# Products of the first token half placed between the two halves of a norm, at five seams of a two-block transformer

## What is computed

```
h = rms_norm(x, g_pre) * (1 + scale) + shift        # modulate
y = sublayer(h)                                      # products with large weights
x = x + res_w * (1 + gate) * rms_norm(y, g_post)     # residual_add
```

## Time and profile before

| | us |
|---|---|
| median of 3 runs (1696.91 to 1699.64) | 1698.38 |
| the profiled execution | 1699.22 |
| its span, first to last instruction | 1697.4 |

### The profile page before, as it was taken

One profiled execution on the slowest core, in us unless ns is written; L12 is line 12 of the kernel. 1 busy time (PEld: TensorE's weight loads), 2 busy tenths in 40 slices (PEclk: granted clock), 3 DMA queues, 4 the chain that ended last, 5 costly groups with the idle time before them and its releaser, 6 DMA issues.

```text
span 1697.4 us, 29607 instructions
## 1 busy us (share of the span) xinstructions
PE 1659.9 (98%) x12344; PEld 1550.8 (91%) x12344; DVE 1266.7 (75%) x1852; ACT 873.8 (51%) x1215; POOL 21.7 (1%) x39
## 2 busy tenths in 40 slices
PE   3999999999999999999999999999999999999998
PEld 3999899988999899989999988999899989989997
DVE  7777889987878677676877765887677686778553
ACT  4555466654544365666464334534355676473432
POOL 0000000000000000000000000000000000000000
PEclk9999999999999999999999999999999999999999
DMA  9878756786777745755558786777945846547542
GB/s 377 319 256 253 268 198 218 208 329 244 295 285 277 294 154 195 223 182 207 208 199 286 284 223 237 246 279 288 287 154 199 221 177 224 212 176 259 198 162 100
DMA packets 71079, 398.80 MB, mean 235 GB/s; under 512 B 8225, under 2 KB 8737, under 8 KB 36385
## 3 DMA queue, kind: packets, MB, share of 16 engines
q1 hardware_dynamic: 67968, 387.43, 65.1%
q0 software_dynamic: 2976, 9.47, 1.6%
HBM read 395.79 MB, written 1.08 MB: 234 GB/s over the span
## 4 chain that ended last, share of the span: by engine, by line
PE 83%; DVE 6%; ACT 5%; DVEq 2%; DMA 1%; issue 1%; SPq 1%; ACTq 0%
PE att L695 19%; PE lin L518 18%; PE lin L519 18%; PE lin L520 18%; DVE lo L1312 3%; ACT hi L922 2%; PE att L802 2%; PE lin L558 1%; PE lin L560 1%; PE lin L568 1%; DVEq L1678 1%; PE att L852 1%; DMA ada_s<-in_ada 1%; ACT work L942 1%; PE pt L829 1%
## 5 line engine op out<-in xcount | busy, mean ns | idle before, releaser
L1312 DVE TENSOR_TENSOR lo<-raw,hi 128x2048 fp32r<-128x2048 f32 x269 | 615.5, 2291 | 254.1 <-ACT hi L922 253.4
L518 PE MATMUL lin<-h_hi,hi 128*128 128x256 f32 x2448 | 688.3, 281 | 1.4 <-DVE work L1673 1.0
L520 PE MATMUL lin<-h_hi,lo 128*128 128x256 f32 x2448 | 683.3, 279 | 0.0
L519 PE MATMUL lin<-h_lo,hi 128*128 128x256 f32 x2448 | 683.3, 279 | 0.0
L922 ACT ACTIVATE hi<-raw 128x2048 fp32r<-128x2048 f32 x269 | 513.3, 1912 | 191.4 <-PE att L695 99.6
L518 PEld LDWEIGHTS lin<-h_hi,hi 128*128 128x128 f32 x2448 | 460.1, 188 | 4.1 <-issue 3.9
L519 PEld LDWEIGHTS lin<-h_lo,hi 128*128 128x128 f32 x2448 | 460.3, 188 | 0.1
L520 PEld LDWEIGHTS lin<-h_hi,lo 128*128 128x128 f32 x2448 | 460.1, 188 | 0.0
L1325 DVE CUSTOM_DVE_ANT_0 ada_w<-ada_w,cs 128x1024 f32<-128x1024 f32 x179 | 217.8, 1219 | 11.9 <-DMA ada_w<-in_ada 11.7
L1162 ACT ACTIVATE work<-lin 128x256 f32<-128x256 f32 x88 | 33.8, 384 | 269.2 <-PE lin L520 268.2
L695 PE MATMUL att<-hi,act_lo 128*128 128x512 f32 x440 | 138.8, 389 | 0.0
(11 more groups left out here) (291 smaller groups left out, 2021.9 us busy)
## 6 DMA issues: line engine op xcount, KB each, us to landing
raw<-in_w SPq DMA_DIRECT2D x269, 1024.0 KB, 4.9
ada_w<-in_ada SPq DMA_DIRECT2D x179, 512.0 KB, 5.1
ada_s<-in_ada SPq DMA_DIRECT2D x13, 512.0 KB, 15.1
bias<-in_bias POOLq DMA_DIRECT2D x16, 256.0 KB, 4.5
ffn_row<-rows POOLq DMA_DIRECT2D x5, 512.0 KB, 9.1
x<-in_x SPq DMA_DIRECT2D x1, 1024.0 KB, 9.8
ra<-rows POOLq DMA_DIRECT2D x2, 512.0 KB, 5.2
dcon<-in_dcon SPq DMA_DIRECT2D x1, 896.0 KB, 7.9
```

Of the source, the lines that this page charges most:

```text
L518: mm(out, w_hi, a_hi, start=start, stop=False, skip_group_check=skip)
L519: mm(out, w_hi, a_lo, start=False, stop=False, skip_group_check=skip)
L520: return mm(out, w_lo, a_hi, start=False, stop=stop, skip_group_check=skip)
L1312: tt(lo[SLOT[c]][:], raw[:, c % RAW, :], hi[SLOT[c]][:].bitcast(F32), ALU.subtract).then_inc(*s_lo.up(c))
```

## The change

Each of the five seams runs the two chunks' `h_hi` products in two parts of 128 columns each. TensorE pads with 2 products instead of 5 and 4, transposes half 0, runs 64 products of 128 columns with the first half of all eight tiles of `h_hi` (`into_h_by_halves`), transposes half 1, runs 64 products with the second half, and then the 32 `h_lo` products as before (`fm_second_half`). ScalarE makes the first half of tiles 0 and 1 between `factor_of_second_half` and `factor_of_x(pre, 1)`; VectorE that of tiles 2 and 3 before `half_of_x` (line 1424) and of tiles 4 to 7 between it and `scaled_x(pre, buf, 1)` (line 1466). Later, `h_first` and `modulated` make only the second half (`left`) of `h_hi`. Cut to its core:

```diff
+            def half_product(out, j, t, c, a, start):
+                b = slice((j * KT + t) * P, (j * KT + t + 1) * P)
+                o = out[:, j * SEQ + a * P:j * SEQ + (a + 1) * P]
+                mm(o, hi[SLOT[c]][:, b], h_hi[:, t, a * P:(a + 1) * P], start=start, stop=False, skip_group_check=True)
+                mm(o, lo[SLOT[c]][:, b], h_hi[:, t, a * P:(a + 1) * P], start=False, stop=False, skip_group_check=True)
+
+            def into_h_by_halves(tag, buf, n, one, two):
+                keep_busy(n)
+                turn_tokens(tag, buf, 0)
+                outs = {}
+                for name in (one, two):
+                    eng.wait_ge(*s_lo.at(AT[name]))
+                    outs[name] = free_bank((AT[name], 0))
+                for t in range(KT):
+                    eng.wait_ge(*(s_first_a if t < 2 else s_first_v).at((tag, t)))
+                    for name in (one, two):
+                        for j in range(2):
+                            half_product(outs[name], j, t, AT[name], 0, t == 0 and j == 0)
+                turn_tokens(tag, buf, 1)
+                return outs
+
+            def fm_second_half(tag, outs, one, two):
+                for tiles in ((0, 2, 1, 3), (4, 5, 6, 7)):
+                    for name in (one, two):
+                        c = AT[name]
+                        for t in tiles:
+                            if name == one:
+                                eng.wait_ge(*(s_h_hi_v if t in (2, 3) else s_h_hi).at((tag, t)))
+                            for j in range(2):
+                                half_product(outs[name], j, t, c, 1, False)
...
                     if a and t % 2:
                         ins.then_inc(*s_across.up((tag, t // 2)))
+                    elif t % 2 and by_halves(tag):
+                        ins.then_inc(*s_half_across.up((tag, t // 2)))
...
-                into_h(l + ".pre1", flat_f, 5, 4)
-                fm_first(l + ".pre1", f"{l}.moba.q0", f"{l}.moba.k0")
+                outs = into_h_by_halves(l + ".pre1", flat_f, 2, f"{l}.moba.q0", f"{l}.moba.k0")
+                fm_second_half(l + ".pre1", outs, f"{l}.moba.q0", f"{l}.moba.k0")
...
+            def first_half_of_h(tag):
+                shift, g, mods = at_of_norm(tag)
+                eng.wait_ge(*s_mods.at(mods))
+                eng.wait_ge(*s_half_across.at((tag, 0)))
+                for t in (0, 1):
+                    act(h_hi[:, t, 0:P], across(t)[:, 0:P], ACT.Identity, bias=mod[:, shift + t:shift + t + 1],
+                        scale=gain[:, g + t:g + t + 1]).then_inc(*s_first_a.up((tag, t)))
+
...
                     factor_of_second_half(post, banks)
+                    first_half_of_h(pre)
                 factor_of_x(pre, post, 1)
...
+            def first_half_of_h(tag, tiles):
+                shift, g, _ = at_of_norm(tag)
+                for t in tiles:
+                    eng.wait_ge(*s_half_across.at((tag, t // 2)))
+                    ts(h_hi[:, t, 0:P], across(t)[:, 0:P], gain[:, g + t:g + t + 1], mod[:, shift + t:shift + t + 1],
+                       ALU.mult, ALU.add).then_inc(*s_first_v.up((tag, t)))
+
...
+                if pre and normed:
+                    first_half_of_h(pre, (2, 3))
                 if pre:
                     half_of_x(pre)
+                    if normed:
+                        first_half_of_h(pre, (4, 5, 6, 7))
                     scaled_x(pre, buf, 1)
```

More of the change, by code:

```diff
@@ L305, in program @@
         s_summed, s_across = signal("summed"), signal("across")
+        s_half_across, s_first_a, s_first_v = signal("half_across"), signal("first_a"), signal("first_v")
         s_hi, s_taken_a, s_silu = signal("hi"), signal("taken_a"), signal("silu")
@@ L409, in across, with by_halves, at_of_norm @@
             return turned_at[t // 2][:, t % 2 * SEQ:(t % 2 + 1) * SEQ]
+        def by_halves(tag):
+            return tag[1:] in (".pre1", ".pre2") or tag == "1.pre0"
+        def at_of_norm(tag):
+            l, n = int(tag[0]), int(tag[-1])
+            return ADA_ONCE + ADA_LAYER * l + 24 * n, 16 + 24 * l + 8 * n, f"{l}.{n}"
         def bank_of(unit):
@@ L568, in fm_first @@
                             ins = mm(outs[i][:, j * SEQ:(j + 1) * SEQ], hi[SLOT[c]][:, b], h_lo[:, t, :], start=False,
+                                     stop=t == 3, skip_group_check=True)
+                    ins.then_inc(*s_mm.up((c, 0), c))
+            def half_product(out, j, t, c, a, start):
[3 more added lines that the diff above has]
+                mm(o, lo[SLOT[c]][:, b], h_hi[:, t, a * P:(a + 1) * P], start=False, stop=False, skip_group_check=True)
@@ new lines, in fm_second_half @@
+            def fm_second_half(tag, outs, one, two):
[7 more added lines that the diff above has]
+                                half_product(outs[name], j, t, c, 1, False)
+                for name in (one, two):
+                    c = AT[name]
+                    for t in (4, 5, 6, 7, 0, 1, 2, 3):
+                        if name == one:
+                            eng.wait_ge(*s_h.at((tag, t)))
+                        for j in range(2):
+                            b = slice((j * KT + t) * P, (j * KT + t + 1) * P)
+                            ins = mm(outs[name][:, j * SEQ:(j + 1) * SEQ], hi[SLOT[c]][:, b], h_lo[:, t, :], start=False,
@@ L893, in _ @@
             for l in map(str, range(LAYERS)):
-                into_h(l + ".pre0", flat_f, 8 if l == "0" else 5, 8 if l == "0" else 4)
-                fm_first(l + ".pre0", f"{l}.up0.0", f"{l}.up0.1")
+                if l == "0":
+                    into_h("0.pre0", flat_f, 8, 8)
+                    fm_first("0.pre0", "0.up0.0", "0.up0.1")
+                else:
+                    outs = into_h_by_halves(l + ".pre0", flat_f, 2, f"{l}.up0.0", f"{l}.up0.1")
+                    fm_second_half(l + ".pre0", outs, f"{l}.up0.0", f"{l}.up0.1")
                 for k in range(2, FT):
@@ L905, in _ @@
                 out_proj(l)
-                into_h(l + ".pre2", rb[:, 0:8, :], 5, 4)
-                fm_first(l + ".pre2", f"{l}.up2.0", f"{l}.up2.1")
+                outs = into_h_by_halves(l + ".pre2", rb[:, 0:8, :], 2, f"{l}.up2.0", f"{l}.up2.1")
+                fm_second_half(l + ".pre2", outs, f"{l}.up2.0", f"{l}.up2.1")
                 for k in range(2, FT):
@@ L1003, in h_first, with from_x @@
                 eng.wait_ge(*s_mods.at(mods))
-                def from_x(out, t):
+                left = slice(P, SEQ) if by_halves(tag) else slice(0, SEQ)
+                def from_x(out, t, tokens=slice(0, SEQ)):
                     eng.wait_ge(*s_across.at((tag, t // 2)))
-                    return act(out, across(t), ACT.Identity, bias=mod[:, shift + t:shift + t + 1],
+                    return act(out, across(t)[:, tokens], ACT.Identity, bias=mod[:, shift + t:shift + t + 1],
                                scale=gain[:, g + t:g + t + 1])
                 for t in (0, 1):
-                    from_x(h_hi[:, t, :], t).then_inc(*s_h_hi.up((tag, t)))
+                    from_x(h_hi[:, t, left], t, left).then_inc(*s_h_hi.up((tag, t)))
                 for t in (6, 7):
@@ L1017, in h_first @@
                         eng.wait_ge(*s_scaled.at((tag, t)))
-                    act(h_hi[:, t, :], turned_tile(t), ACT.Copy).then_inc(*s_h_hi.up((tag, t)))
+                    act(h_hi[:, t, left], turned_tile(t)[:, left], ACT.Copy).then_inc(*s_h_hi.up((tag, t)))
                 for t in (0, 1, 2, 3):
@@ L1399, in modulated, with from_x @@
                     shift = ADA_ONCE + ADA_LAYER * int(tag[0]) + 24 * int(tag[-1])
-                def from_x(out, t):
+                left = slice(P, SEQ) if by_halves(tag) else slice(0, SEQ)
+                def from_x(out, t, tokens=slice(0, SEQ)):
                     eng.wait_ge(*s_across.at((tag, t // 2)))
-                    return ts(out, across(t), gain[:, g + t:g + t + 1], mod[:, shift + t:shift + t + 1],
+                    return ts(out, across(t)[:, tokens], gain[:, g + t:g + t + 1], mod[:, shift + t:shift + t + 1],
                               ALU.mult, ALU.add)
                 for t in (2, 3):
-                    from_x(h_hi[:, t, :], t).then_inc(*s_h_hi_v.up((tag, t)))
+                    from_x(h_hi[:, t, left], t, left).then_inc(*s_h_hi_v.up((tag, t)))
                 for t in (4, 5):
```

## The result

The changed kernel takes 1716.99 us, median of four runs (1715.66 to 1717.98), against 1698.83 for the kernel before: a ratio of 1.011, 95% interval 1.0095 to 1.0125. It is slower by 18 us. The forecast was 1716.2, in the likeliest case.

What follows compares the result with a forecast made beforehand. TensorE's queue was taken as the bound; per seam 7.1 us of new products replace 3.4 of padding and wait, 0.45 comes back: 3.55 more, 17.8 over five seams, forecast 1716.2 us; range 1695 to 1722 (0.81).

Steps and rivals of the forecast that it cites:

- likeliest case: All five seams: weight loads set the product price, 0.111 us; 1716.2 us, own range 1712 to 1722, chance 0.71.
- The price of a 128-column product: TensorE's narrow products in the seams: 0.111 us each, bounded by the weight load, against 0.118 for 256 columns.
- Padding 5 to 2: Ahead of the first transposes in 1.pre1: they start 1.3 us earlier, just after VectorE's data, and the clock does not fall.
- the 17.8 of the sum: Forecast loss in us over five seams, taking 3.55 us more for each from seam 1.pre1.
- First tile, first product: ScalarE's first half tile in 1.pre1: first product 0.71 us after its start, 2.4 us after line 695's last product.
- The inserted waits on VectorE: First-half products: line 1466 ends by 1251.1 instead of 1249.35, yet TensorE asks only at 1253.5, so no cost.
- Second transposes to first product: In the seam, between the two halves' products: 1.1 us instead of 1.24, with 0.1 less for the narrower tile.
- Second half and h_lo: End of the seam: 64 second-half products take 7.1 us instead of 7.55; h_lo products stay at 3.73.
- Plain f32 price: Rival: narrow fp32r products run as two matmuls, 0.22 us each; 17.5 us more per seam, about 1786; chance 0.08.
- the price near break of even: Rival: narrow products cost 0.080 to 0.086 us, loads partly hidden; 1696 to 1700 us, no difference; chance 0.10.
- Columns alone: Rival: streamed columns set the price, 0.062 us; 1.8 us less per seam, 9 in all, about 1689; chance 0.11.
- The point of decision at 0.083: Price in us per 128-column product in seam 1.pre1 below which the change gains.

Runs made afterwards that it cites:

- e1: Changed kernel, its 128-column products using only 64 of the 128 columns of each weight tile; 1702.1 us (one run) beside 1699.8 for the kernel before.
- e2: Changed kernel, its 128-column products streaming only 64 token columns past whole 128-column weights; 1776.2 us.
- e3: Kernel before with the change's padding alone (2 calls instead of 5, none instead of 4), products as before; 1705.0 against 1699.8 us, ratio 1.0031.
- e6: Kernel before with chunk v0 first at two mixer seams, token half 0 stationary, 256 weight columns streaming in the wait; 1696.76 against 1699.23 us, ratio 0.9984.

## Why the prediction was right, point by point

- **The price of a 128-column product** (taken: 0.111; ends 0.108 and 0.118). Measured 0.112, and now shown to be the weight load (e1, e2), not only argued from rows. Of these, were no evidence for a load, and that they gave the right number was luck: the padding, of the same type, costs 0.216 for 256 columns, and half of that, by the columns alone, is 0.108 for 128. What pointed at the load were the two loads of the earlier trace rows. The Trainium skill ("TensorE: Matmul & The Clock Gate", section "LDWEIGHTS (loading the stationary operand)") says that a load's time goes with the number of weight columns, columns/1.2 in ns; by that an estimated 107 ns for 128 and 53 for 64. The loads that start 0.11 apart agree, and those of e1 at 0.05 to 0.06 don't contradict it, though there the stream of 128 columns may set the pace as well. At 1.2 GHz, in e2, they are 0.21 apart, so the formula fits the upper level alone. The 81 ns per matmul that the same page of the Trainium skill gives for N=128 (section "Back-to-back issue gap") was not met: 112 was measured for these operands.
- **Padding 5 to 2**: first transposes at 1.08 in 1.pre1, as worked out (1.1). But I took this seam for all five. At 0.pre2 and 1.pre2 VectorE's half 0 comes later, which the padding had covered. In 0.pre2 it is there 1.49 us after line 746's last product, in 1.pre1 at 1.02, and TensorE waited 0.30 for it. These two seams took 21.89 and 21.75 instead of 21.4, which is why five seams cost 18.4 and not the 17.8 of the sum. And the padding is not free to drop by itself, which I had not seen: e3. I excluded a fall of the clock because TensorE has almost no pause. It did not fall, but the reason does not carry: in e2 TensorE has hardly a pause either, and it fell.
- **First tile, first product**: forecast 2.4, measured 2.25. ScalarE starts the tiles 0.1 sooner (1256.22, ahead of the recorded end of line 989), and the first product follows 0.59 behind their start, not 0.71; the narrower activations are shorter (two in 0.79).
- **The inserted waits on VectorE cost nothing as long as the products take that long**: so it was; TensorE has no stop between 1256.81 and 1263.98, although the quarters came later than before.
- **Second transposes to first product**: 1.1 forecast, 1.01 measured.
- **Second half and h_lo**: 7.1 and 3.73 forecast; 7.20 (1264.99 to 1272.19) and 3.79 measured. The seam: 3.55 more forecast, 3.52 measured. That it is so close is in part chance: the start of the first product was 0.17 too late in the sum and the second transposes 0.09 too long, the two halves and h_lo 0.23 too short.
- **The rivals.** Plain f32 price and the price near break of even fell to the rows above. "Columns alone" fell as well, and its price was wrong: I had the third chunk's *weights* late next, by up to 1.0 us. e1, with products at 0.06, shows that at three seams of five the first chunk's *bank* is late, behind ScalarE's splits and a table load, and that the clock falls at these stops. By e1's 1702.1 (one run, with a part of the products left out) this case would have ended near no change instead of 9 us faster. The point of decision at 0.083 holds for the two mixer seams at most.

## What to carry to other kernels

Before moving work into a wait, ask what it costs there: a product with half the streamed columns and the same weights is not half a product when each brings its own weight load; here it cost 0.112 of 0.118. If only one half of the tokens is ready, put that half on the stationary side and stream the full width of the other operand (e6: 2.5 us won at two seams), or leave the wait alone. And padding that looks like waste can hold the clock (e3: 5 us lost without it): take it out by itself once, and read the granted clock of the stretch.

## What was not expected of the hardware

In e2 TensorE hardly stopped: weight loads cover 31.78 of the 32.00 us from 608.00 on, and all of the 27.27 us at half clock. Yet the clock fell to 1.2 GHz and stayed there through the narrow products and beyond them (the last one starts at 634.07), while products of 128 columns at the same distance (0.112) in the changed kernel kept 2.4 GHz. Busy, as the profile counts it, did not hold the clock here; what makes the difference was not tried further.
